# Attention scores as two one-pass products of stacked high and low parts, in a two-block model kernel

## The reference

```python
logits = einsum('bhqd,bhkd->bhqk', qi, k) * scale      # scale = DH_B ** -0.5
logits = logits + (Fi[..., :, None] - F[..., None, :]) # F = cumsum(log sigmoid(f))
logits = where(q_pos[:, None] >= k_pos[None, :], logits, -inf)
p = softmax(logits, axis=-1)
out = einsum('bhqk,bhkd->bhqd', p, v)
```

## Time and profile before

| | |
|---|---|
| time, median of 3 runs | 2905.71 us (2902.89 to 2908.36) |
| the profiled execution's own time | 2906.73 us |
| its span | 2904.9 us |
| busy PE / DVE / ACT / POOL | 2785.0 / 1792.1 / 1035.5 / 26.2 us |
| granted PE clock over the span | 0.981 |
| attention loop | about 465 to 755 us of the span |

### The profile page before, as it was taken

One profiled execution on the slowest core, in us unless ns is written; L12 is line 12 of the kernel. 1 busy time (PEld: TensorE's weight loads), 2 busy tenths in 40 slices (PEclk: granted clock), 3 DMA queues, 4 the chain that ended last, 5 costly groups with the idle time before them and its releaser, 6 DMA issues.

```text
span 2904.9 us, 35093 instructions
## 1 busy us (share of the span) xinstructions
PE 2785.0 (96%) x12345; PEld 2205.4 (76%) x12345; DVE 1792.1 (62%) x2747; ACT 1035.5 (36%) x1629; POOL 26.2 (1%) x44
## 2 busy tenths in 40 slices
PE   6999999999999989999999999999999899999996
PEld 3468887777788866788877778787788688888884
DVE  6855675555698757445564738483967777335454
ACT  3032222444332355422243533443422622234224
POOL 0000000000000000000000000000000000000000
PEclk9999999999999989999999999999999999999998
DMA  9966552222466647365522222225566365333331
GB/s 342 356 209 222 189 190 82 78 73 73 131 204 203 229 134 252 138 219 189 189 80 88 94 80 87 73 94 177 194 223 217 105 214 189 94 95 101 124 123 58
DMA packets 240189, 451.25 MB, mean 155 GB/s; under 512 B 23848, under 2 KB 45818, under 8 KB 235436
## 3 DMA queue, kind: packets, MB, share of 16 engines
q1 hardware_dynamic: 237236, 440.80, 46.1%
q0 software_dynamic: 2304, 8.39, 0.8%
q10 hardware_dynamic: 504, 0.17, 0.0%
HBM read 422.01 MB, written 27.30 MB: 155 GB/s over the span
## 4 chain that ended last, share of the span: by engine, by line
PE 84%; DVE 6%; ACT 3%; issue 2%; DVEq 2%; DMA 2%; ACTq 1%; SPq 1%
PE ps L1325 20%; PE ps L1328 20%; PE ps L1331 20%; PE ps L1553 4%; PE ps L1338 3%; PE ps L1344 3%; PE ps L1341 2%; PE ps L1781 2%; PE ps L1815 1%; PE ps L1812 1%; PE ps L1295 1%; PE ps L1300 1%; PE ps L1297 1%; PE ps L1689 1%; PE ps L1698 1%
## 5 line engine op out<-in xcount | busy, mean ns | idle before, releaser
L1325 PE MATMUL ps<-op_hi,w_hi 128*128 128x512 f32 (+2 forms) x2800 | 784.2, 399 | 21.9 <-ACT op_hi L926 7.6
L1838 DVE TENSOR_TENSOR w_lo<-w_raw,w_hi 128x512 fp32r<-128x512 f32 (+2 forms) x672 | 440.9, 662 | 560.0 <-ACT w_hi L688 311.2
L1331 PE MATMUL ps<-op_hi,w_lo 128*128 128x512 f32 (+2 forms) x2800 | 756.8, 390 | 4.4 <-DVE w_lo L1838 4.4
L1328 PE MATMUL ps<-op_lo,w_hi 128*128 128x512 f32 (+2 forms) x2800 | 759.5, 391 | 0.0
L1325 PEld LDWEIGHTS ps<-op_hi,w_hi 128*128 128x128 f32 (+1 forms) x2800 | 520.5, 190 | 140.5 <-issue 26.2
L1331 PEld LDWEIGHTS ps<-op_hi,w_lo 128*128 128x128 f32 (+1 forms) x2800 | 528.2, 189 | 116.6 <-DVE w_lo L1838 5.6
L1328 PEld LDWEIGHTS ps<-op_lo,w_hi 128*128 128x128 f32 (+1 forms) x2800 | 529.5, 189 | 112.9 <-issue 0.3
L688 ACT ACTIVATE w_hi<-w_raw 128x512 fp32r<-128x512 f32 (+2 forms) x416 | 242.9, 592 | 612.4 <-PE ps L1331 447.2
L1861 DVE SCALAR_TENSOR_TENSOR acc<-a_raw,vec,acc 128x512 f32<-128x512 f32 x525 | 381.7, 746 | 17.5 <-DMA a_raw<-in_w_ada 14.5
L713 ACT ACTIVATE w_hi<-w_raw 128x512 fp32r<-128x512 f32 x288 | 181.7, 632 | 581.7 <-PE ps L1331 449.6
L2566 DVE TENSOR_TENSOR w_lo<-w_raw,w_hi 128x512 fp32r<-128x512 f32 x128 | 83.6, 687 | 62.0 <-ACT w_hi L1188 56.6
(11 more groups left out here) (278 smaller groups left out, 2446.9 us busy)
## 6 DMA issues: line engine op xcount, KB each, us to landing
a_raw<-in_w_ada SPq DMA_DIRECT2D x216, 512.0 KB, 4.0
w_raw<-in_w_in_e SPq DMA_DIRECT2D x160, 512.0 KB, 4.7
w_raw<-in_w_in SPq DMA_DIRECT2D x96, 512.0 KB, 4.8
arena<-in_w_ada SPq DMA_DIRECT2D x72, 512.0 KB, 7.0
w_raw<-in_w_in_o SPq DMA_DIRECT2D x64, 512.0 KB, 4.4
w_raw<-in_w_out SPq DMA_DIRECT2D x32, 512.0 KB, 4.8
w_raw<-in_w_out_e SPq DMA_DIRECT2D x32, 512.0 KB, 5.1
w_raw<-in_w_out_o SPq DMA_DIRECT2D x32, 512.0 KB, 3.8
```

The source lines that it names most:

```text
L1325: mm(ps[0:m, bank + j, 0:tok], hi[:, cols], B.op_hi[:, k, 0:tok], start=first, stop=False)
L1328: mm(ps[0:m, bank + j, 0:tok], hi[:, j * P:j * P + m], B.op_lo[:, k, 0:tok], start=False, stop=False)
L1331: last = mm(ps[0:m, bank + j, 0:tok], lo[:, j * P:j * P + m], B.op_hi[:, k, 0:tok], start=False, stop=last_t)
L1838: V.tensor_tensor(B.w_lo[:, c % RING, 0:width], B.w_raw[:, c // 2 % RAW, c % 2, 0:width], B.w_hi[:, c % RING, 0:width].bitcast(f32), ALU.s ...
```

## The change

The score product takes float32r operands: the stationary operand holds the queries of a head stacked, high part in the head's own 64 rows and low part in the other 64; the moving operand is first the high part of the keys (in both halves), then the low part (in both halves). Two one-pass products into the same bank take the place of the float32 one. All three operands are staged for each head in `stage` (two buffers, one over `acc`, one in the arena).

- POOL makes for each head the high parts of queries and keys in the own rows (two copies) and the low part of the keys there (a subtraction); it no longer clears the other rows. For head 0 it does so before the attention, as soon as `acc` is free.
- ACT makes the high part of the keys in the other rows (`stage_high`), at the start of a unit with u % 4 == 1, for the next head.
- DVE makes the low part of the queries and of the keys in the other rows (`stage_low`), one each behind the low part of the tile in the units with u % 4 == 1 and 2, for the next head.
- ACT copies the turned probabilities of unit u-1 ahead of the exponentials of unit u, except in output units, where the order stays.
- At the end of a turn ACT copies the four banks out (`left`), and one Gelu or Silu over all of TMP (`activated`) follows at the end of the next unit, behind its high part. `gated` moves from u % 16 == 1 to u % 16 == 3 (the last one stays at u = 65).

```diff
@@ pool_program
-    queries = at(AT_QST, 2, S)
-
-    pool.wait_ge(sem("mixing"), HEADS_A)
     for h in range(HEADS_B):
-        rows, others = (slice(DH_B * (x % 2), DH_B * (x % 2 + 1)) for x in (h, h + 1))
-        if h < 2:
-            nc.gpsimd.memset(queries[others, h, :], 0.0)
-        if h >= 2:
+        stage = B.stage[h % 2]
+        own, _ = head_rows(h)
+        q, k = head_source(B, h)
+        if h == 0:
+            pool.wait_ge(sem("part_summed"), o)
+        elif h == 1:
+            pool.wait_ge(sem("mixing"), HEADS_A)
+            pool.wait_ge(sem("mixed"), HEADS_A)
+        else:
             pool.wait_ge(sem("scores"), 4 * (h - 1) + 1)
-        nc.gpsimd.tensor_copy(queries[rows, h % 2, :], B.Y[rows, 8 + h // 2, :])
-        nc.gpsimd.drain().then_inc(sem("queries_in"), 1)
+        nc.gpsimd.tensor_copy(stage[own, ST_Q, :], q)
+        nc.gpsimd.tensor_copy(stage[own, ST_HIGH, :], k)
+        nc.gpsimd.drain().then_inc(sem("stage_high"), 1)
+        nc.gpsimd.tensor_tensor(stage[own, ST_LOW, :], k, stage[own, ST_HIGH, :].bitcast(mybir.dt.float32),
+                                mybir.AluOpType.subtract)
+        nc.gpsimd.drain().then_inc(sem("stage_own_low"), 1)
@@ attention_scalar
+    stage_high(0)
     for u in range(UNITS + 1):
...
+        if u % 4 == STAGE_AT and u // 4 + 1 < HEADS_B:
+            stage_high(u // 4 + 1)
+        outputs = (u - 11) // 8 if u >= 11 and u % 8 == 3 else None
+        if outputs is not None:
+            exponents(u)
+            pair_out(outputs)
+            taken(u - 1)
+        else:
+            if u >= 1:
+                taken(u - 1)
+            if u < UNITS:
+                exponents(u)
         high_to(min(u + 3, UNITS + 4))
+        if u >= 16 and u % 16 == 0:
+            activated(u // 16 - 1)
         if u % 16 == 15:
...
+            left(u // 16)
@@ attention_tensor
-            pe.wait_ge(sem("queries_in"), s // 4 + 1)
-            mm(ps[:, 4 + s % 2, 0:P * (b + 1)], at(AT_QST, 2, S)[:, half, b * P:(b + 1) * P],
-               keys[:, pair, 0:P * (b + 1)], start=True, stop=True).then_inc(sem("scores"), 1)
+            if b == 0:
+                pe.wait_ge(sem("stage_other_high"), s // 4 + 1)
+                pe.wait_ge(sem("stage_own_low"), s // 4 + 1)
+                pe.wait_ge(sem("stage_other_low"), 2 * (s // 4 + 1))
+            queries = B.stage[half][:, ST_Q, b * P:(b + 1) * P]
+            high, low = (B.stage[half][:, k, 0:P * (b + 1)] for k in (ST_HIGH, ST_LOW))
+            mm(ps[:, 4 + s % 2, 0:P * (b + 1)], queries, high, start=True, stop=False)
+            mm(ps[:, 4 + s % 2, 0:P * (b + 1)], queries, low, start=False, stop=True).then_inc(sem("scores"), 1)
@@ vector_program, before the mixing
+            stage_low(B, dve, 0)
@@ stage_low (new)
+STAGE_AT = 1
+def stage_low(B, dve, h, parts=(0, 1)):
+    dve.wait_ge(B.sem("stage_high"), h + 1)
+    own, other = head_rows(h)
+    q, k = head_source(B, h)
+    for part, x, high in [((ST_Q, q, ST_Q), (ST_LOW, k, ST_HIGH))[n] for n in parts]:
+        B.nc.vector.tensor_tensor(B.stage[h % 2][other, part, :], x,
+                                  B.stage[h % 2][own, high, :].bitcast(mybir.dt.float32),
+                                  mybir.AluOpType.subtract).then_inc(B.sem("stage_other_low"), 1)
@@ attention_vector
         low_to(min(u + 3, UNITS + 4))
-        if u >= 16 and u % 16 == 1:
+        if STAGE_AT <= u % 4 <= STAGE_AT + 1 and u // 4 + 1 < HEADS_B:
+            stage_low(B, dve, u // 4 + 1, (u % 4 - STAGE_AT,))
+        if u >= 16 and u % 16 == 3 or u == UNITS + 1:
             gated(u // 16 - 1)
```

More of the change, by code:

```diff
@@ L225, in __init__ @@
         self.acc = sb("acc", [P, 2, 2, GC])
+        acc_at = nc.sbuf_base - 4 * 4 * GC
         self.const = sb("const", [P, N_CONST])
@@ L233, in __init__ @@
         self.arena = sb("arena", [P, ARENA])
+        arena_at = nc.sbuf_base - 4 * ARENA
+        self.stage = [nc.alloc_sbuf_tensor_at("stage_even", [P, 3, S], f32r, offset=acc_at),
+                      nc.alloc_sbuf_tensor_at("stage_odd", [P, 3, S], f32r, offset=arena_at + 4 * AT_STAGE)]
         self.ps = nc.alloc_psum_tensor("ps", [P, 8, GC], f32)
@@ L594, with head_rows, head_source @@
 LAG = 3
+def head_rows(h):
+    own, other = (slice(DH_B * (x % 2), DH_B * (x % 2 + 1)) for x in (h, h + 1))
+    return own, other
+def head_source(B, h):
+    own, _ = head_rows(h)
+    return B.Y[own, 8 + h // 2, :], B.at(AT_K, 8, S)[own, h // 2, :]
 def pool_program(B, pool):
@@ L608, in pool_program @@
             .then_inc(B.va_in[b % RAW], 16)
[L610 to L612 removed]
+    o = ordinal(FIRST["ua"])
+    o += halves_before(o)
     for h in range(HEADS_B):
[L614 to L621 removed]
+        stage = B.stage[h % 2]
+        own, _ = head_rows(h)
+        q, k = head_source(B, h)
[5 more added lines that the diff above has]
+        else:
+            pool.wait_ge(sem("scores"), 4 * (h - 1) + 1)
+        nc.gpsimd.tensor_copy(stage[own, ST_Q, :], q)
[4 more added lines that the diff above has]
+        nc.gpsimd.drain().then_inc(sem("stage_own_low"), 1)
     n = FIRST["wo1"]
@@ L1117, in high_to, with exponents, taken, left @@
             made += 1
+    def exponents(u):
+        w = P * (u % 4 + 1)
+        act.wait_ge(sem("logits"), u + 9)
+        Act(logit[:, u % 2, 0:w], logit[:, u % 2, 0:w], ACT.Exp, bias=B.small[:, 8 + u % 2:9 + u % 2],
+            accum_out=B.small[:, 16 + u % 16:17 + u % 16]).then_inc(sem("probs"), 1)
+    def taken(u):
+        w = P * (u % 4 + 1)
+        act.wait_ge(sem("p_turned"), u + 3)
+        act.wait_ge(sem("pv"), u + 1)
+        Act(p_t[:, u % 2, 0:w], ps[:, 6, 0:w], ACT.Copy).then_inc(sem("p_taken"), 1)
+    def left(turn):
+        act.wait_ge(sem("w_used"), kc + KT * (turn + 1))
+        act.wait_ge(sem("tmp_free"), turn + 1)
+        for b in range(4):
+            Act(at(TMP, 4, S)[:, b, :], ps[:, b, :], ACT.Copy).then_inc(sem("gate_left"), 1)
+    def activated(turn):
+        nc.scalar.drain()
+        Act(at(TMP, 4, S), at(TMP, 4, S), ACT.Silu if turn >= 2 else ACT.Gelu)
+        nc.scalar.drain().then_inc(sem("tmp_full"), 1)
     def pair_out(q):
@@ L1122, in pair_out, with stage_high @@
         Act(Y[:, 8 + q, :], ps[:, 6, :], ACT.Copy).then_inc(sem("o_taken"), 1)
-    for u in range(UNITS + 1):
[L1125 to L1138, removed]
+    def stage_high(h):
+        if h == 0:
+            o = ordinal(FIRST["ua"])
+            act.wait_ge(sem("part_summed"), o + halves_before(o))
+        elif h == 1:
+            act.wait_ge(sem("mixing"), HEADS_A)
+            act.wait_ge(sem("mixed"), HEADS_A)
+        else:
+            act.wait_ge(sem("scores"), 4 * (h - 1) + 1)
+        _, other = head_rows(h)
+        _, k = head_source(B, h)
+        Act(B.stage[h % 2][other, ST_HIGH, :], k, ACT.Copy).then_inc(sem("stage_other_high"), 1)
+    stage_high(0)
+    for u in range(UNITS + 1):
+        if u % 4 == STAGE_AT and u // 4 + 1 < HEADS_B:
[5 more added lines that the diff above has]
+            taken(u - 1)
+        else:
+            if u >= 1:
+                taken(u - 1)
+            if u < UNITS:
+                exponents(u)
         high_to(min(u + 3, UNITS + 4))
+        if u >= 16 and u % 16 == 0:
+            activated(u // 16 - 1)
         if u % 16 == 15:
[L1142 to L1148, removed]
+            left(u // 16)
     high_to(UNITS + 4)
@@ L1685, in attention_tensor @@
         if s < UNITS:
-            pair, half, b = s // 8, s // 4 % 2, s % 4
+            half, b = s // 4 % 2, s % 4
             pe.wait_ge(sem("score_slots"), s + 1)
-            pe.wait_ge(sem("queries_in"), s // 4 + 1)
-            mm(ps[:, 4 + s % 2, 0:P * (b + 1)], at(AT_QST, 2, S)[:, half, b * P:(b + 1) * P],
-               keys[:, pair, 0:P * (b + 1)], start=True, stop=True).then_inc(sem("scores"), 1)
+            if b == 0:
[6 more added lines that the diff above has]
+            mm(ps[:, 4 + s % 2, 0:P * (b + 1)], queries, low, start=False, stop=True).then_inc(sem("scores"), 1)
         if s >= 2:
```

5 lines of the change are left out of this document (3 added, 2 removed).

## The result

The changed kernel takes 2923.56 us (median of 6 runs, 2919.35 to 2930.07), the kernel before beside it 2905.89 (2902.89 to 2910.86): a ratio of 1.0059, 95% interval 1.0048 to 1.0070. It is slower by 0.6%, 17.7 us, where I had forecast 2903. The profiled execution took 2930.07, its span is 2928.3.

What follows compares the result with a forecast made beforehand. PE was taken to bound the kernel, the DVE and ACT chain nearly as long afterwards. First turn -2.6, later turns 0, loop end +0.2: -2.4 on 2906.7, 2904.3, less 1.0 for the median, say 2903 us; range 2893 to 2914.

Steps and rivals of the forecast that it cites:

- the part on the chain: DVE and ACT work per head: chain 15.2 us against PE's 15.4; POOL's staging done in time, about 15 us available.
- rival (2): POOL and DVE exclude each other in the attention loop: slower, 2912 to 2915 us; chance 0.28.
- 0.61 of a copy: One POOL meeting costs DVE 0.61 us a head, making the chain 15.8 against PE's 15.4.
- steeper branch: POOL's subtraction gets in ahead of DVE's mask: 1.2 us a head and 2920 us.
- The clock: Granted clock of the attention loop, read as 1.00 in the profile before the change.
- the prices: Score pairs 0.455 us (512 columns) and 0.24 (256); PE's work 15.4 a head; each `stage_low` subtraction 0.69.
- The working of the turn end: Behind each turn end, 3.5 us less PE work is given back whole: three turns give 0, error 1.5 each.
- the first turn: First turn of the loop: gains 3.5 us less 0.2 at the start and 0.75 at one output unit, 2.6.
- PE start 1 to 2 us earlier: Loop start: POOL's copy no longer waited for lets PE start earlier, to wait for the same transfer.
- Rival (1): The DVE and ACT chain has more room than counted: 9 to 14 us gained, 2892 to 2897; chance 0.30.
- Rival (3): The scores don't get cheaper at all: about 3 to 5 us lost; chance under 0.05.
- 0.2 us a head: Cost of POOL and DVE meetings from which rival (2) decides; the chain's room per head was also 0.2.

Runs made afterwards that it cites:

- runs 1 and 2: Run 1 is `no_pool`; run 2 is the changed kernel with POOL clearing the same rows by four memsets a head for heads 2 to 15: 2903.63 us.
- no_pool: The changed kernel without POOL's two copies and subtraction for heads 2 to 15: 2903.16 us, ratio 0.9987 against the kernel before.
- pool_no_subtraction: The changed kernel without POOL's subtraction for heads 2 to 15, its two copies kept: 2910.97 us, ratio 1.0015 against the kernel before.
- no_stage: The changed kernel without any staging on POOL, ACT and DVE for heads 2 to 15: 2892.42 us, ratio 0.9942 against the kernel before.
- turn_only: The kernel before with only the new order of ACT and the new turn ends, float32 scores: 2901.12 us, ratio 0.9980.

## Why the prediction was wrong

The failing step stands in the part on the chain: POOL's copies and subtraction "start with the last score of the head before and have four units, some 15 us". That priced POOL's work by when it is done, and it is done in time: no wait of PE names POOL. What it does to DVE meanwhile was put into rival (2), with 0.28, and there at "0.61 of a copy" a head. The runs show the rival's mechanism (runs 1 and 2) and its steeper branch: the subtraction does get in ahead of the mask, which the rival had at 1.2 us a head and 2920. Without POOL's three instructions the time is 2903.2, so a term that the forecast had at nothing measures 20.4 us.

- **The size of a meeting.** In the timeline of DVE and POOL above, the mask loses 0.94 and `stage_low` 0.45, 1.4 for a head, of which PE sees about 1.0. From the score product at 580.11 to that at 615.33 lie two heads with an output unit and no fall of the clock: 35.2 us, against 33.2 for the same half turn in `no_pool` (568.73 to 601.92). In `pool_no_subtraction` it is 33.7 (576.17 to 609.90), so of 1.0 a head the subtraction is 0.75 and the copies 0.27. I had looked for the danger at DVE's longest operations; the dearest place was its shortest, since the mask stands ahead of the maximum, the exponentials and the scaling.
- **A wait that I didn't count.** PE's product of probabilities and values waits for DVE's scaling of the unit before (L2621), which stands behind the maximum. It is the largest releaser of L1770, 10.2 us in the changed kernel and 4.8 in `no_pool`. In my working DVE's lateness reached PE only through exponentials, `pair_out` and the copy.
- **The clock.** I took 1.00 for the whole loop. Read microsecond by microsecond, it stands at its lower level (0.50, that is 1.2 GHz) for some 27 us of the changed kernel's loop, in six stretches and in each turn; in `no_pool` for some 10 us, in two stretches. Half turns with a fall take 38.05 and 37.31 (500.69 to 538.74, 655.79 to 693.10) instead of the 35.22 without. Over the two loops (468 to 770 and 466 to 748) the same number of PE instructions, 1396, is busy 269.5 us in the changed kernel and 261.5 in `no_pool`, and PE is idle 32.6 and 20.5. So of the 20 us between the loops 12 are idle time of PE, and 8 are products that took longer at the lower clock. The 8 went with POOL's instructions, as the 12 did; that the waits bring the falls about is not shown, as no run here changes the clock alone.
- **What was right: the prices.** Pairs of 512 and 256 columns take 0.46 and 0.24 (0.455 and 0.24 forecast), a head without outputs and turn end 15.42 in `no_pool` (482.93 to 498.35; 15.4 forecast), and 64 rows of `stage_low` cost as much as the low part's 128, 0.69. The working of the turn end can be held against `no_pool`, which is the changed kernel without the meetings. Its timeline behind u = 16, whose score product starts at 531.03:

```profile
540.57 0.51 ACT L1154 ACTIVATE arena<-arena,small 128x256 f32<-128x256 f32 x1
...
543.17 0.61 DVE L2604 SCALAR_TENSOR_TENSOR arena<-arena,ps 128x384 f32<-128x384 f32 x1
...
547.53 0.75 DVE L2604 SCALAR_TENSOR_TENSOR arena<-arena,ps 128x512 f32<-128x512 f32 x1
...
550.18 0.57 ACT L1181 ACTIVATE Y<-ps 128x512 f32<-128x512 f32 x1
...
550.90 0.52 PE L1787 MATMUL ps<-const,arena 128*128 128x128 f32 x3 [1.63 <-ACT Y L1181]
...
555.79 0.35 DVE L2604 SCALAR_TENSOR_TENSOR arena<-arena,ps 128x128 f32<-128x128 f32 x1 [0.22 <-issue]
```

Exponentials of 17 start at 9.5 (10.3 forecast), L2514's heirs for 18, 19 and 20 at 12.1, 16.5 and 24.8 (12.4, 16.8, 25.0), `pair_out` is done at 19.7 (20.0); PE waits 1.6 there and 1.3 in smaller waits before it, where I had one wait of 2.9. Turns come out at 70.9 and 71.0 (71.4 forecast), and the time at 2903.2 (2903 forecast). The agreement of the totals is partly luck: the first turn of `no_pool` takes 65.4 us where mine had 63.7, and the later ones are each 0.4 to 0.5 better. Nor does PE start 1 to 2 us earlier, as I had it: the loop starts at 465.63 in `no_pool` and 468.15 in the changed kernel, 465.68 before.
- **Rival (1)**, more room in the chain, is refuted by `no_stage`: only without any staging does the time reach 2892, the range that this rival had with it. **Rival (3)** fell with the first rows of the section on the result.
- **Why 0.28 was too little.** The rows of before have POOL's copy only beside L2514, which reads PSUM, and it slowed nothing. That is no evidence against the rival: L2602 stays at 0.75 beside POOL's copy in the changed kernel as well. The rule that I cited, of the Trainium skill (SBUF — State Buffer, Who interferes with whom), speaks of a DVE instruction with two SBUF inputs. By that rule the trace agrees on all counts: the two-tile instructions wait (0.29 to 1.23), POOL's own wait in turn (1.29 to 3.09), L2602 with one tile and PSUM doesn't, and POOL's instructions without a read (521 ns each) stop nobody. With the rule taken at its word, the question left was who gets in first, and the order of the queues answered it: POOL is released by the last score product of a head, and in the next microseconds DVE has three two-tile instructions.

The forecast of "0.2 us a head" as the point from which the rival decides was right in kind: the half turn of `no_pool` is only 0.5 us shorter than the same one before (33.7, 569.68 to 603.41), so there was no room to take the meetings.

## What to carry to other kernels

An instruction that is given to an idle engine isn't free for that: ask what else it holds, and list the instructions of the busy engine that it can lie beside, not only the wait that it must meet. Here 44 us of work on an engine that is idle 98% of the time cost 20 us, and the same engine writing in the same places cost nothing. Edits that are tried as one should be timed apart. The turn ends gain 5.3 us. The one-pass scores add at the most 8.7 to that (`turn_only` 2901.1 to `no_stage` 2892.4), and the staging on ACT and DVE alone takes 10.7, so they bring no gain even where POOL costs nothing (`no_pool`, 2903.2). A kernel with the float32 scores, the new order and the new turn ends is the version to keep.

## What the hardware did that I had not expected

The granted clock fell to its lower level six times inside the loop, five times directly behind a wait of PE of 2.0 to 2.8 us and once, at 618, behind one of 0.99. Windows of 6 us in the changed kernel around two of them (the column ahead of the last two is the clock):

```profile
519.00:525.00 6.00, 5.26 (x20) 4.71 (x21) 2.16 (x7) 3.13 (x8) 0.00 (x0) 0.56 0.31 93
525.00:531.00 6.00, 6.00 (x30) 5.03 (x29) 2.60 (x7) 1.74 (x5) 0.00 (x0) 0.87 0.11 39
561.00:567.00 6.00, 5.74 (x21) 5.07 (x22) 3.62 (x4) 1.61 (x3) 0.00 (x0) 0.50 0.32 102
```

and the timeline of PE there:

```profile
519.48 0.70 PE L1785 MATMUL ps<-const,arena 128*128 128x128 f32 x3 [1.97 <-ACT Y L1179]
...
560.99 0.87 PE L1785 MATMUL ps<-const,arena 128*128 128x128 f32 x3 [2.62 <-ACT Y L1179]
...
564.49 2.06 PE L1392 MATMUL ps<-op_hi,w_hi 128*128 128x512 f32 x4
```

Four products of 512 columns take 2.06 us here, and 1.18 beside 577.25 at full clock. The length of the wait alone doesn't decide. A wait of 1.97 us was followed by the fall at 519.48 and by a clock of 1.00 at 598.90, and in `no_pool` one of 1.6 by 1.00 at 550.90 and by 0.57 from 693 to 699. Where the clock falls behind a wait, the half turns compared above are 2 to 3 us longer.

Second, the exclusion works both ways and without regard to length: POOL's 1.29 us became 3.09 behind a DVE instruction of 2.29, and a mask of 0.29 became 1.23 behind POOL.
